# Weight subtractions of a two-block transformer kernel, from VectorE to GpSimd

## The chip, the cores and the metric

The kernel runs on one core of one Trainium2 chip. The metric is the device time of one execution in microseconds (us). Its engines are TensorE (PE in the profile, with PEld for its weight loads), VectorE (DVE), ScalarE (ACT), GpSimd (POOL) and SyncE (SP), which here issues the DMA transfers. Each runs its own row of instructions in order, and they meet through semaphores.

## The reference, cut to what matters

One sequence of 256 tokens with 1024 features goes through two blocks, in float32. Shortened:

```python
# block 1
h = rmsnorm(x, norm_mix)
fq, fk, fv, ff, gq, gk, gv, gb, ga, gz, sq, sk, sv, gates = split(h @ w_in)
ya = fox_attention(rmsnorm(fq), rmsnorm(fk), fv, log_sigmoid(ff + bias))    # softmax attention, decaying
yb = rmsnorm(gated_delta_rule(silu(conv(gq, gk, gv)), gb, ga)) * silu(gz)   # chunks of 64, triangular solve
yc = stick_breaking_attention(sq, sk, sv)
x = x + (g0 * (ya @ w_oa) + g1 * (yb @ w_ob) + g2 * (yc @ w_oc)) @ w_out    # g = sigmoid(gates + bias)
x = x + memory_cross_attention(rmsnorm(x), rmsnorm(mem), w_mq, w_mkv, w_mo)
a, b = split(causal_conv3(rmsnorm(x) @ w_up) + conv_b)                      # 2 x 2816 channels
x = x + (silu(a) * b) @ w_down
# block 2
q, k, v, g, gb, gc, u = split(rmsnorm(x) @ w_in_2)
x = x + concat(silu(g) * groupnorm(retention(rotary(q), rotary(k), v)), gb * conv(gc * u)) @ w_o_2
x = x + moe(rmsnorm(x))               # 64 experts in 8 groups, 2 per token, each 1024 -> 512 -> 1024
return rmsnorm(x, final)
```

## The kernel before, in words

Data stay in SBUF with features on the 128 partitions and the 256 tokens beside each other. The dense weights of everything but the experts are cut into 101 *units* (the list `UNITS`, in the order of use), each 128x2048 float32, 1 MB. Examples: `gq0`, `fv1` (projections), `ga00` (gates), `oa_0` (output projections), `U12` (a column of 128 channels of both halves of `w_up`), `D4` (256 rows of `w_down`), `o200` to `o211` (`w_o_2`).

A product is made in a faster number format, fp32r, in three passes. Each weight W is split as W = high + low, where high is W rounded to fp32r, and each input likewise; then high·high, high·low and low·high are added in PSUM (the function `product`, lines 281 to 283). A unit takes 48 matmuls. Four engines work at a unit one after the other:

1. SyncE issues its load into one of `RAW` = 5 buffers (`raw`), once the unit five before it is multiplied (`done`).
2. ScalarE rounds it into one of `HIGH` = 3 buffers `w_high` (line 871, in `ahead`), once the unit three before it is multiplied, and raises the semaphore `w_high`.
3. VectorE subtracts: `w_low` = `raw` − `w_high`, written over `raw` (line 1354, in `lows`), and raises the semaphore `w_low`.
4. TensorE waits for `w_low` in `parts` and multiplies.

Steps 2 and 3 have no queue of their own. Calls of `ahead(name)` and `lows(name)` stand by hand between the other work of ScalarE and VectorE, and each makes the units up to the one that is named. So a subtraction starts when VectorE's row comes to it, even if its rounded half has long been there, and what stands behind it in the row starts 2.29 us later.

VectorE's other work before the experts: `normalise` (`inverse_root`, then eight multiplications and four low parts `h_low`), roots and products per head, the convolutions' taps, and `split` (a cast to the high part, then a subtraction for the low part, lines 1344 and 1345). In the feed-forward stage a channel column c goes: `up(c)` on TensorE; the tap copy `f_y` on ScalarE (line 1183), which then rounds a unit; taps on VectorE (line 1683); Silu on ScalarE (line 1190); `product(c)` on VectorE, which is `f_act`, the cast `act_high` and the subtraction `act_low`. VectorE takes `product(c - 1)` behind the taps of c. TensorE's order is `up(2j+2)`, `up(2j+3)`, `down(j)`, and `down(j)` needs columns 2j and 2j+1. GpSimd has no work of the program.

Behind the dense units come the router and the 64 experts, whose weights (6 MB each) SyncE loads in three sets of buffers. Expert 0 is loaded in part earlier; `load_gate_up(1, 1)` waits until the last unit is multiplied.

Of the kernel before, what the change touches and what calls it, by code (L numbers as in the profile page):

```python
# [14 lines left out]
ALU = mybir.AluOpType  # L15
# [10 lines left out]
D = 1024  # L26
# [52 lines left out]
def program(nc, c1_in, c2_in, sm_in, rb_in, x_in, mem_in, dense_in, rows_w_in, router_w_in, experts_in, out):  # L79
    with ExitStack() as ctx:  # L80
# [1225 lines left out]
        def _(dve):  # L1306
# [39 lines left out]
            H_PARTS = (h_high, h_low)  # L1346
            w_next = [0]

            def lows(name, n=0):

                while w_next[0] <= min(ORDER[name] + n, LAST):
                    w = UNITS[w_next[0]]
                    dve.wait_ge(sem("w_high"), w_next[0] + 1)
                    V.tensor_tensor(low(w), raw[:, place(w), :], high(w).bitcast(F32),  # L1354
                                    ALU.subtract).then_inc(sem("w_low"), 1)
                    w_next[0] += 1

            dve.wait_ge(sem("consts_loaded"), 32)
            dve.wait_ge(sem("x_loaded"), 16)
            lows(UNITS[0])  # L1360
            normalise("mix", x, A["h"], "norm_mix", H_PARTS)
            lows("gk0")

# [6 lines left out]
            for nm, first in (("gq", 0), ("gk", H), ("gv", 2 * H)):  # L1370
                for u in range(2):
                    ps = half(proj.wait(dve, f"{nm}{u}"))
                    nu += 1
                    dve.wait_ge(sem("gdn_tap"), nu)
                    for s in (1, 2, 3):
                        for i in range(2):
                            ch = first + 2 * u + i
                            o = conv_dst(ch)[:, s:T]
                            ins = V.scalar_tensor_tensor(o, ps[:, i, 0:T - s], S_("gdn_conv", 4 * ch + 3 - s), o,
                                                         ALU.mult, ALU.add)  # L1380
                            if s == 3:
# [5 lines left out]
                    lows(f"{nm}{u}", HIGH)  # L1387

# [15 lines left out]
                            ALU.subtract).then_inc(sem("gdn_tail"), 1)  # L1404
            lows("fk1")


            for hd in range(H):
# [5 lines left out]
                                ALU.mult).then_inc(sem("gdn_k"), 1)  # L1414
            lows("fv0")

# [8 lines left out]
                            ALU.mult).then_inc(sem("gdn_beg"), 1)  # L1425
            lows("fv1")

            for q in range(2):
# [10 lines left out]
                aux.release(dve, f"decay{q}")  # L1439
            lows("sq0")  # L1440

            for nm, gain in (("q", A["st"][:, 24:25]), ("k", S_("fox_k"))):
                for hd in range(H):
                    rs = sq[:, (0 if nm == "q" else H) + hd, :]
                    inverse_root(rs)
                    o = A[f"fox_{nm}"][:, hd, :]
                    V.scalar_tensor_tensor(o, o, gain, rs, ALU.mult, ALU.mult).then_inc(sem(f"fox_{nm}n"), 1)
                lows("sq1" if nm == "q" else "sk0")

            for t in range(TT):  # L1450
                for q in range(2):
# [8 lines left out]
                    aux.release(dve, f"kk{t}{q}")  # L1460
            lows("sk1")
            V.tensor_tensor(A["gdn_qk"][:, :, 0, :], A["gdn_qk"][:, :, 0, :], A["eg"], ALU.mult)
# [55 lines left out]
            for lv in range(len(LEVELS)):  # L1518
                if lv < 5:
                    lows(("sv0", "sv1", "ga00", "ga01", "oa_0")[lv])  # L1520
# [75 lines left out]
            sbout = lambda hd: head_out("spv", hd, yc, "yc")  # L1596
            state(0); sb_keep(0); sb_keep(1); lows("ga11"); mix("a", 0, 0); vnew(1); mix("a", 0, 1); sb_masked(0)
            state(1); sb_masked(1); lows("oa_1"); sbout(0); mix("a", 1, 0); lows("gc00"); sbout(1); vnew(2); mix("a", 1, 1)
            lows("gc01")
            sb_keep(2); sb_keep(3); state(2); sb_masked(2); sb_masked(3); vnew(3); lows("oc_0"); sbout(2); sbout(3)  # L1600
            lows("gc10")
            mix("c", 0, 0); lows("gc11"); mix("c", 0, 1)
            for hd in range(H):
                if hd == 2:
                    lows("oc_1")
# [6 lines left out]
            lows("gb00")  # L1612
            mix("c", 1, 0); lows("gb01"); mix("c", 1, 1)
            lows("gb10")
            mix("b", 0, 0); lows("gb11"); mix("b", 0, 1); lows("ob_1")
            mix("b", 1, 0); lows("out01"); mix("b", 1, 1); lows("out10")

# [9 lines left out]
            residual(("out00", "out01"), "x1")  # L1627
            lows("out11")
            normalise("mem", M["mem"], M["mem"], "norm_mem", hm)
            lows("mk0")  # L1630
            residual(("out10", "out11"), "x1", 2)
            lows("mq0")
            normalise("xq", x, M["mem"], "norm_xq", H_PARTS)
            lows("mv0")
            V.tensor_scalar(M["st"][:, 24:25], S_("mq"), SCALE, None, ALU.mult)
# [7 lines left out]
            mem_norm("k", S_("mk"), range(H))  # L1643
            lows("mv1")
            mem_norm("q", M["st"][:, 24:25], (0, 1))
            lows("mo_0")

# [17 lines left out]
            mem_norm("q", M["st"][:, 24:25], (3,))  # L1665
            mem_max(2); mout(0); mem_norm_p(2); mem_max(3); mout(1); lows("mo_1"); mem_norm_p(3); mout(2); mout(3)
            lows("U0")
            residual(("mo0", "mo1"), "x2")
            lows("U1")
            residual(("mo2", "mo3"), "x2", 2)  # L1670


            normalise("ffn", x, M["mem"], "norm_ffn", H_PARTS)
            lows("U2")

# [19 lines left out]
            for c in range(FC + 1):  # L1695
                if c < FC:
                    taps(c)
                if c:
                    product(c - 1)
                if c < FC:  # L1700
                    lows(f"U{c}", HIGH)
                if c % 2 and c < FC:
                    lows(f"D{c // 2}")
            for b in range(4):
# [6 lines left out]

            lows("q21")
            normalise("n1", x, R["cat"], "norm1", H_PARTS)
            lows("v20")
            dve.wait_ge(sem("c2_loaded"), 16)
# [12 lines left out]
            rotary("q")  # L1728
            lows("gc20")
            rotary("k")  # L1730
            lows("gc21")

# [8 lines left out]
            for hd in range(H):  # L1741
                ret_decay(hd)
                if hd % 2:
                    lows(f"u2{hd // 2}")
            lows("gb20")
            def conv_in(u):
# [9 lines left out]
            for hd in range(H):  # L1756
# [4 lines left out]
                dve.sem_inc(sem("ret_d"), 1)  # L1761
            lows("gb21")
            conv_in(1)
            lows("g20")

# [9 lines left out]
            for hd in range(H):  # L1775
# [3 lines left out]
                link(V.scalar_tensor_tensor(o, o, S_("ret_gn", hd), rs, ALU.mult, ALU.mult))  # L1779
            lows("g21")  # L1780
            for u in range(2):
# [4 lines left out]
                split(cat[0][:, c, :], cat[1][:, c, :], o).then_inc(sem("cat"), 2)  # L1786
            lows("o200")
            for hd in range(H):
                if hd == 2:
                    lows("o201")  # L1790
# [3 lines left out]
            lows("o210")  # L1794
            residual(("o200",), "x4")
            lows("o211")
            residual(("o201", "o210", "o211"), "x4", 1)

# [128 lines left out]
            for k in range(DC):  # L1927
                V.scalar_tensor_tensor(h[:, k, :], x[:, k, :], S_("final", k), sq[:, 0, :], ALU.mult,
                                       ALU.mult).then_inc(sem("result"), 1)


# [217 lines left out]
```

## Time and profile before

| | us |
|---|---|
| median of 3 runs | 1758.27 (1757.1 to 1759.49) |
| the profiled execution, its own time | 1757.1 |
| its span in the profile | 1755.3 |
| TensorE busy | 1354.2 |
| VectorE busy | 647.4 |
| ScalarE busy | 482.1 |
| GpSimd busy | 0.2 |

A row of the page's or the trace's groups names the line of the program, the engine, the operation, `out<-in` by the program's names, and the shapes; `x` is a count. Behind a bar stand the group's busy time, the mean of one in ns, and the idle time of its engine just before, with what ended it (`<-`). In a timeline the first number is the start in us from the span's start, the second the length; what stands in brackets is idle time before the instruction and its releaser. The columns of a stretch are its length, then for each engine busy us and instructions, the granted TensorE clock as a share of full speed, the busy share of the DMA engines and GB/s. A matmul is shown with a length of 0.28 us, but since matmuls overlap, the distance between two starts is the time one takes.

### The profile page before, as it was taken

What the parts mean: (1) busy time and instruction counts of PE and PEld (TensorE: products, weight loads), DVE (VectorE), ACT (ScalarE), POOL (GpSimd) and SP (SyncE); (2) the same over time, 40 slices, a digit from 0 to 9 for tenths busy, and PEclk for the clock granted to TensorE, in tenths of its full rate; (3) what the DMA queues carried; (4) which work ended last, traced back from release to release, by engine and by line L of the source; (5) the groups of instructions that cost most, each with busy time, mean ns of one, the idle gap of its engine ahead of it and who ended that gap; (6) DMA issues with size and microseconds to landing.
All of it is one profiled execution on the core that took longest, in us unless ns stands there. A gap on an engine that the chain in (4) does not pass through costs nothing.

```text
span 1755.3 us, 31165 instructions
## 1 busy us (share of the span) xinstructions
PE 1354.2 (77%) x13670; PEld 1064.1 (61%) x13670; DVE 647.4 (37%) x993; ACT 482.1 (27%) x783; POOL 0.2 (0%) x4
## 2 busy tenths in 40 slices
PE   7998899999799998997766566666665666566665
PEld 6987899989699998987433333333333333333333
DVE  6785635858677776574100010101000100010002
ACT  5773366446455444442000000000000000000001
POOL 0000000000000000000000000000000000000000
PEclk9999999999999999997988897888887988888888
DMA  7432023444265553475899999999999999999995
GB/s 285 166 121 97 25 97 108 158 167 144 73 231 180 182 191 121 148 307 217 366 431 431 430 430 430 430 431 430 431 431 432 432 430 430 431 432 430 430 430 223
DMA packets 34773, 517.27 MB, mean 295 GB/s; under 512 B 3858, under 2 KB 3986, under 8 KB 4882
## 3 DMA queue, kind: packets, MB, share of 16 engines
q1 hardware_dynamic: 34706, 516.32, 72.2%
q8 instruction: 50, 0.82, 0.2%
q14 instruction: 17, 0.14, 0.0%
HBM read 515.25 MB, written 1.05 MB: 294 GB/s over the span
## 4 chain that ended last, share of the span: by engine, by line
PE 45%; DMA 40%; DVE 10%; ACT 3%; issue 1%; SPq 0%; DVEq 0%; ACTq 0%
DMA e_gu<-experts 39%; PE psum L770 11%; PE psum L281 9%; PE psum L282 9%; PE psum L283 9%; DVE all_sq L1322 3%; DVE w_low L1354 2%; PE psum L487 1%; PE psum L340 1%; ACT w_high L871 1%; PE psum L471 1%; PE psum L806 0%; DMA w_raw<-dense 0%; DVE m_sq L1322 0%; PE psum L779 0%
## 5 line engine op out<-in xcount | busy, mean ns | idle before, releaser
L770 PE MATMUL psum<-e_gu,x_xt 128*32 128x256 f32 x4096 | 298.7, 456 | 245.9 <-DMA e_gu<-experts 231.2
L770 PEld LDWEIGHTS psum<-e_gu,x_xt 128*32 128x32 f32 x4096 | 147.2, 130 | 389.3 <-DMA e_gu<-experts 254.2
L281 PE MATMUL psum<-h_high,w_high 128*128 128x256 f32 x1024 | 296.0, 289 | 24.2 <-DVE h_low L1332 15.2
L282 PE MATMUL psum<-h_low,w_high 128*128 128x256 f32 x1024 | 291.6, 285 | 0.0
L283 PE MATMUL psum<-h_high,w_low 128*128 128x256 f32 x1024 | 291.4, 285 | 0.0
L1354 DVE TENSOR_TENSOR w_low<-w_raw,w_high 128x2048 fp32r<-128x2048 f32 x101 | 230.8, 2289 | 56.6 <-ACT w_high L871 50.5
L281 PEld LDWEIGHTS psum<-h_high,w_high 128*128 128x128 f32 x1024 | 196.9, 192 | 27.7 <-issue 16.3
L871 ACT ACTIVATE w_high<-w_raw 128x2048 fp32r<-128x2048 f32 x101 | 193.1, 1914 | 68.8 <-PE psum L283 58.3
L282 PEld LDWEIGHTS psum<-h_low,w_high 128*128 128x128 f32 x1024 | 197.3, 193 | 0.4 <-issue 0.2
L283 PEld LDWEIGHTS psum<-h_high,w_low 128*128 128x128 f32 x1024 | 197.2, 193 | 0.0
L1914 DVE COPY x_yb<-psum 128x256 f32<-128x256 f32 x64 | 27.2, 425 | 429.5 <-PE psum L806 429.5
L1912 DVE TENSOR_TENSOR x_act<-x_sil,psum 128x128 f32<-128x128 f32 x64 | 18.3, 285 | 349.1 <-ACT x_sil L1294 349.1
L806 PE MATMUL psum<-e_dn,x_actT 128*32 128x256 f32 x2048 | 123.8, 382 | 28.8 <-ACT x_actT L1298 28.8
L1294 ACT ACTIVATE x_sil<-psum 128x128 f32<-128x128 f32 x64 | 17.9, 279 | 444.7 <-PE psum L770 444.7
L1296 ACT ACTIVATE x_scat<-psum 128x256 f32<-128x256 f32 x64 | 24.6, 384 | 305.0 <-PE psum L796 303.2
L806 PEld LDWEIGHTS psum<-e_dn,x_actT 128*32 128x32 f32 x2048 | 60.0, 109 | 75.5 <-ACT x_actT L1298 42.5
L812 PE MATMUL psum<-x_scat,x_yb 32*128 32x256 f32 x1024 | 73.3, 400 | 35.0 <-DVE x_yb L1914 35.0
L812 PEld LDWEIGHTS psum<-x_scat,x_yb 32*128 32x128 f32 x1024 | 46.2, 184 | 67.2 <-DVE x_yb L1914 65.8
L779 PE MATMUL psum<-x_s,x_htok 128*128 128x128 f32 x512 | 64.3, 286 | 2.7 <-DVE x_s L1863 2.7
L779 PEld LDWEIGHTS psum<-x_s,x_htok 128*128 128x128 f32 x512 | 61.2, 199 | 7.9 <-issue 5.0
L1322 DVE RECIPROCAL all_sq<-all_sq 128x256 f32<-128x256 f32 (+1 forms) x27 | 53.6, 1987 | 23.7 <-ACTq L850 20.3
L281 PE MATMUL psum<-act_high,w_high 128*128 128x256 f32 x176 | 49.5, 281 | 1.5 <-DVE act_low L1345 1.5
(403 smaller groups left out, 1808.3 us busy)
## 6 DMA issues: line engine op xcount, KB each, us to landing
e_gu<-experts SPq DMA_DIRECT2D x64, 4096.0 KB, 23.8
e_dn<-experts SPq DMA_DIRECT2D x64, 2048.0 KB, 25.3
w_raw<-dense SPq DMA_DIRECT2D x101, 1024.0 KB, 4.8
all_c<-c SPq DMA_DIRECT2D x1, 2099.5 KB, 15.8
r_c<-c SPq DMA_DIRECT2D x1, 1344.0 KB, 5.7
all_x<-x_t SPq DMA_DIRECT2D x1, 1024.0 KB, 5.0
m_mem<-mem_t SPq DMA_DIRECT2D x1, 1024.0 KB, 4.8
out_t<-all_h SPq DMA_DIRECT2D x4, 256.0 KB, 2.6
```

Of the source, the lines that this page charges most:

```text
L281: mm(ps, w[0], src[0], start=start, stop=False, **kw)
L282: mm(ps, w[0], src[1], start=False, stop=False, **kw)
L283: return mm(ps, w[1], src[0], start=False, stop=stop, **kw)
L770: last = mm(half(psum[32 * s:32 * s + 32, GU_BANK[j % 2], 0:256], P), X["xt"][:, k, CAP * j:CAP * (j + 1)], expert_gu[PLACE[j]][:, k, :, s ...
L779: last = mm(psum[:, 4 + c // 4, (c % 4) * P:(c % 4 + 1) * P], X["htok"][:, t, c * P:(c + 1) * P], X["s"][:, t, :], start=(t == 0), stop=(t ...
L806: last = mm(psum[32 * s:32 * s + 32, 7, 0:256], X["actT"][:, CAP * c:CAP * (c + 1)], expert_dn[PLACE[j]][:, c, s * T:(s + 1) * T], start=( ...
L812: last = mm(psum[:, s, d * T:(d + 1) * T], X["yb"][32 * s:32 * s + 32, d * P:(d + 1) * P], X["scat"][32 * s:32 * s + 32, :], start=False, ...
L871: ac(high(w), raw[:, place(w), :], ACT.Copy).then_inc(sem("w_high"), 1)
L1296: ac(X["scat"], psum[:, 7, 256:512], ACT.Copy).then_inc(sem("scatter_kept"), 1)
L1322: link(V.reciprocal(rs, rs))
L1354: V.tensor_tensor(low(w), raw[:, place(w), :], high(w).bitcast(F32), ALU.subtract).then_inc(sem("w_low"), 1)
L1914: V.tensor_copy(X["yb"], psum[:, 7, 0:256]).then_inc(sem("e_y"), 1)
```

## The change

The subtraction of step 3 leaves VectorE. GpSimd gets a row of its own that holds nothing else: for each unit in order it waits for `w_high` and subtracts, with the same operands and the same semaphore behind it. The function `lows` and all of its calls go; where a call stood between two parts of one loop or one list, these are joined. TensorE's, ScalarE's and SyncE's rows stay. The diff, of whose calls taken out a few stand for all:

```diff
-            w_next = [0]
-
-            def lows(name, n=0):
-
-                while w_next[0] <= min(ORDER[name] + n, LAST):
-                    w = UNITS[w_next[0]]
-                    dve.wait_ge(sem("w_high"), w_next[0] + 1)
-                    V.tensor_tensor(low(w), raw[:, place(w), :], high(w).bitcast(F32),
-                                    ALU.subtract).then_inc(sem("w_low"), 1)
-                    w_next[0] += 1
...
-            lows(UNITS[0])
             normalise("mix", x, A["h"], "norm_mix", H_PARTS)
-            lows("gk0")
...
-                lows("sq1" if nm == "q" else "sk0")
...
-                if c < FC:
-                    lows(f"U{c}", HIGH)
-                if c % 2 and c < FC:
-                    lows(f"D{c // 2}")
...
-            residual(("o200",), "x4")
-            lows("o211")
-            residual(("o201", "o210", "o211"), "x4", 1)
+            residual(("o200", "o201", "o210", "o211"), "x4")
...
+        @block.gpsimd
+        def _(pool):
+
+            for n, name in enumerate(UNITS):
+                pool.wait_ge(sem("w_high"), n + 1)
+                nc.gpsimd.tensor_tensor(low(name), raw[:, place(name), :], high(name).bitcast(F32),
+                                        ALU.subtract).then_inc(sem("w_low"), 1)
```

On VectorE, in the feed-forward stage, the row before held a subtraction behind each column (`f_y` are the taps, `f_act` to `act_low` the product):

```order
L1354 TENSOR_TENSOR w_low<-w_raw,w_high 128x2048
L1683 SCALAR_TENSOR_TENSOR f_y<-psum,all_sm,f_y 128x255 x2
L1683 SCALAR_TENSOR_TENSOR f_y<-psum,all_sm,f_y 128x254 x2
L1693 TENSOR_TENSOR f_act<-f_sa,f_y 128x256
L1344 CAST act_high<-f_act 128x256
L1345 TENSOR_TENSOR act_low<-f_act,act_high 128x256
L1354 TENSOR_TENSOR w_low<-w_raw,w_high 128x2048
```

The row of the changed kernel at the same place:

```order
L1647 SCALAR_TENSOR_TENSOR f_y<-psum,all_sm,f_y 128x255 x2
L1647 SCALAR_TENSOR_TENSOR f_y<-psum,all_sm,f_y 128x254 x2
L1657 TENSOR_TENSOR f_act<-f_sa,f_y 128x256
L1344 CAST act_high<-f_act 128x256
L1345 TENSOR_TENSOR act_low<-f_act,act_high 128x256
```

The two subtractions are gone, and the five others follow each other as they did.

On VectorE, between the first attention's keys (`a_fox_k`) and the triangular solve, before:

```order
L1322 RECIPROCAL all_sq<-all_sq 128x256
L1447 SCALAR_TENSOR_TENSOR a_fox_k<-a_fox_k,all_sm,all_sq 128x256
L1354 TENSOR_TENSOR w_low<-w_raw,w_high 128x2048
L1458 TENSOR_TENSOR a_kd<-psum,a_t 128x256 x8
L1354 TENSOR_TENSOR w_low<-w_raw,w_high 128x2048
L1462 TENSOR_TENSOR a_gdn_qk<-a_gdn_qk,a_eg 128x4x256
L1467 TENSOR_TENSOR all_sq<-a_kd,all_c_58 128x1024
```

And now:

```order
L1322 RECIPROCAL all_sq<-all_sq 128x256
L1430 SCALAR_TENSOR_TENSOR a_fox_k<-a_fox_k,all_sm,all_sq 128x256
L1440 TENSOR_TENSOR a_kd<-psum,a_t 128x256 x8
L1443 TENSOR_TENSOR a_gdn_qk<-a_gdn_qk,a_eg 128x4x256
L1448 TENSOR_TENSOR all_sq<-a_kd,all_c_58 128x1024
```

The chain to the first solve (`all_sq` is the masked matrix that it starts from) is two subtractions shorter. All 101 of them stand in GpSimd's row:

```order
L1881 TENSOR_TENSOR w_low<-w_raw,w_high 128x2048 x101
```

## Rows read from the trace of the kernel before

**Rows 1.** Page, part 1: busy us (share of the span) x instructions.
```profile
PE 1354.2 (77%) x13670; PEld 1064.1 (61%) x13670; DVE 647.4 (37%) x993; ACT 482.1 (27%) x783; POOL 0.2 (0%) x4
```

**Rows 2.** Stretches; stretch, its length, then columns as headed.
```profile
core 0: us, PE busy (x) PEld busy (x) DVE busy (x) ACT busy (x) POOL busy (x), PEclk, DMA share, GB/s
0.00:800.00 800.00, 738.84 (x5706) 712.04 (x5707) 539.09 (x676) 404.84 (x551) 0.20 (x4) 0.97 0.44 155
480.00:660.00 180.00, 179.26 (x1515) 179.06 (x1514) 133.34 (x185) 88.95 (x99) 0.00 (x0) 1.00 0.56 192
800.00:1755.00 955.00, 615.41 (x7965) 352.03 (x7963) 108.30 (x318) 77.30 (x232) 0.00 (x0) 0.85 0.96 412
```

**Rows 3.** Page, part 4: chain that ended last, shares by line.
```profile
DMA e_gu<-experts 39%; PE psum L770 11%; PE psum L281 9%; PE psum L282 9%; PE psum L283 9%; DVE all_sq L1322 3%; DVE w_low L1354 2%; PE psum L487 1%; PE psum L340 1%; ACT w_high L871 1%; PE psum L471 1%; PE psum L806 0%; DMA w_raw<-dense 0%; DVE m_sq L1322 0%; PE psum L779 0%
```

**Rows 4.** Timeline of TensorE; start us, us, engine line op out<-in.
```profile
567.52 0.28 PE L281 MATMUL psum<-act_high,w_high 128*128 128x256 f32 x1
...
573.20 0.28 PE L281 MATMUL psum<-h_high,w_high 128*128 128x256 f32 x1
```

**Rows 5.** Waits of TensorE, 0 to 810: us in total, times, longest us.
```profile
PE psum L281 <- DVE w_low L1354: 13.7, 7, 3.1
...
PE psum L281 <- DVE act_low L1345: 1.5, 1, 1.5
```

**Rows 6.** Groups by line and form, VectorE, 0 to 810; busy us, mean ns.
```profile
L1354 DVE TENSOR_TENSOR w_low<-w_raw,w_high 128x2048 fp32r<-128x2048 f32 x101 | 230.8, 2289 | 56.6 <-ACT w_high L871 50.5 <-DVE a_s L1571 0.6 <-DVE all_x L1622 0.5
...
L1345 DVE TENSOR_TENSOR act_low<-f_act,act_high 128x256 fp32r<-128x256 f32 x22 | 9.4, 426 | 0.8
L1693 DVE TENSOR_TENSOR f_act<-f_sa,f_y 128x256 f32<-128x256 f32 x22 | 9.4, 425 | 7.8 <-ACT f_sa L1190 7.0 <-DVE f_y L1683 0.8
...
L1344 DVE CAST act_high<-f_act 128x256 fp32r<-128x256 f32 x22 | 6.5, 294 | 0.8
```

**Rows 7.** Timeline of VectorE, first attention.
```profile
120.74 1.75 DVE L1322 RECIPROCAL all_sq<-all_sq 128x256 f32<-128x256 f32 x1
...
122.92 2.28 DVE L1354 TENSOR_TENSOR w_low<-w_raw,w_high 128x2048 fp32r<-128x2048 f32 x1
...
139.67 2.29 DVE L1354 TENSOR_TENSOR w_low<-w_raw,w_high 128x2048 fp32r<-128x2048 f32 x1
```

**Rows 8.** Timeline of VectorE, ahead of o200.
```profile
761.35 2.29 DVE L1354 TENSOR_TENSOR w_low<-w_raw,w_high 128x2048 fp32r<-128x2048 f32 x1
...
771.73 2.28 DVE L1354 TENSOR_TENSOR w_low<-w_raw,w_high 128x2048 fp32r<-128x2048 f32 x1
```

**Rows 9.** Timeline of ScalarE, feed-forward stage.
```profile
562.04 1.02 ACT L1183 ACTIVATE f_y<-psum,all_sm 128x256 f32<-128x256 f32 x2 [3.70 <-PE psum L283]
562.95 1.91 ACT L871 ACTIVATE w_high<-w_raw 128x2048 fp32r<-128x2048 f32 x1
564.75 0.41 ACT L1190 ACTIVATE f_sa<-f_y 128x256 f32<-128x256 f32 x1
```

**Rows 10.** Timeline of VectorE, feed-forward stage.
```profile
565.27 0.43 DVE L1693 TENSOR_TENSOR f_act<-f_sa,f_y 128x256 f32<-128x256 f32 x1 [0.32 <-ACT f_sa L1190]
565.73 0.29 DVE L1344 CAST act_high<-f_act 128x256 fp32r<-128x256 f32 x1
566.06 0.43 DVE L1345 TENSOR_TENSOR act_low<-f_act,act_high 128x256 fp32r<-128x256 f32 x1
566.40 2.29 DVE L1354 TENSOR_TENSOR w_low<-w_raw,w_high 128x2048 fp32r<-128x2048 f32 x1
```

**Rows 11.** Timelines of ScalarE and VectorE, the first instructions.
```profile
13.14 0.47 ACT L848 ACTIVATE all_sq<-psum,all_c 128x256 f32<-128x256 f32 x1 [0.25 <-PE psum L340]
...
11.52 2.29 DVE L1354 TENSOR_TENSOR w_low<-w_raw,w_high 128x2048 fp32r<-128x2048 f32 x1 [11.52 <-ACT w_high L871]
13.77 1.75 DVE L1322 RECIPROCAL all_sq<-all_sq 128x256 f32<-128x256 f32 x1
```

**Rows 12.** Timeline of VectorE, a cast out of PSUM.
```profile
190.46 0.42 DVE L1344 CAST ya_high<-psum 128x256 fp32r<-128x256 f32 x1
```

More of the change, by code:

```diff
@@ L1386, in _ @@
                     proj.release(dve, f"{nm}{u}")
-                    lows(f"{nm}{u}", HIGH)
             dve.wait_ge(sem("late_consts_loaded"), 16)
@@ L1404, in _ @@
                             ALU.subtract).then_inc(sem("gdn_tail"), 1)
-            lows("fk1")
             for hd in range(H):
@@ L1414, in _ @@
                                 ALU.mult).then_inc(sem("gdn_k"), 1)
-            lows("fv0")
             ps = aux.wait(dve, "tok")
@@ L1425, in _ @@
                             ALU.mult).then_inc(sem("gdn_beg"), 1)
-            lows("fv1")
             for q in range(2):
@@ L1439, in _ @@
                 aux.release(dve, f"decay{q}")
-            lows("sq0")
             for nm, gain in (("q", A["st"][:, 24:25]), ("k", S_("fox_k"))):
@@ L1460, in _ @@
                     aux.release(dve, f"kk{t}{q}")
-            lows("sk1")
             V.tensor_tensor(A["gdn_qk"][:, :, 0, :], A["gdn_qk"][:, :, 0, :], A["eg"], ALU.mult)
@@ L1518, in _ @@
             for lv in range(len(LEVELS)):
-                if lv < 5:
-                    lows(("sv0", "sv1", "ga00", "ga01", "oa_0")[lv])
                 between()
@@ L1596, in _ @@
             sbout = lambda hd: head_out("spv", hd, yc, "yc")
[L1597 to L1602, printed above, removed]
+            state(0); sb_keep(0); sb_keep(1); mix("a", 0, 0); vnew(1); mix("a", 0, 1); sb_masked(0)
+            state(1); sb_masked(1); sbout(0); mix("a", 1, 0); sbout(1); vnew(2); mix("a", 1, 1)
+            sb_keep(2); sb_keep(3); state(2); sb_masked(2); sb_masked(3); vnew(3); sbout(2); sbout(3)
+            mix("c", 0, 0); mix("c", 0, 1)
             for hd in range(H):
-                if hd == 2:
-                    lows("oc_1")
                 rs = sq[:, hd, :]
@@ L1611, in _ @@
                 split(yb[0][:, hd, :], yb[1][:, hd, :], o).then_inc(sem("yb"), 1)
[L1612 to L1616, printed above, removed]
+            mix("c", 1, 0); mix("c", 1, 1)
+            for hf in range(2):
+                for p in range(2):
+                    mix("b", hf, p)
             def residual(names, done, n=0):
@@ L1627, in _ @@
             residual(("out00", "out01"), "x1")
-            lows("out11")
             normalise("mem", M["mem"], M["mem"], "norm_mem", hm)
-            lows("mk0")
             residual(("out10", "out11"), "x1", 2)
-            lows("mq0")
             normalise("xq", x, M["mem"], "norm_xq", H_PARTS)
-            lows("mv0")
             V.tensor_scalar(M["st"][:, 24:25], S_("mq"), SCALE, None, ALU.mult)
@@ L1643, in _ @@
             mem_norm("k", S_("mk"), range(H))
-            lows("mv1")
             mem_norm("q", M["st"][:, 24:25], (0, 1))
-            lows("mo_0")
             def mem_max(hd):
@@ L1665, in _ @@
             mem_norm("q", M["st"][:, 24:25], (3,))
[L1666 to L1670, printed above, removed]
+            mem_max(2); mout(0); mem_norm_p(2); mem_max(3); mout(1); mem_norm_p(3); mout(2); mout(3)
+            residual(("mo0", "mo1", "mo2", "mo3"), "x2")
             normalise("ffn", x, M["mem"], "norm_ffn", H_PARTS)
-            lows("U2")
             def taps(c):
@@ L1709, in _ @@
                 dve.sem_inc(sem("x3"), 1)
-            lows("q21")
             normalise("n1", x, R["cat"], "norm1", H_PARTS)
-            lows("v20")
             dve.wait_ge(sem("c2_loaded"), 16)
@@ L1728, in _ @@
             rotary("q")
-            lows("gc20")
             rotary("k")
-            lows("gc21")
             def ret_decay(hd):
@@ L1742, in _ @@
                 ret_decay(hd)
-                if hd % 2:
-                    lows(f"u2{hd // 2}")
-            lows("gb20")
             def conv_in(u):
@@ L1761, in _ @@
                 dve.sem_inc(sem("ret_d"), 1)
-            lows("gb21")
             conv_in(1)
-            lows("g20")
             for u in range(2):
@@ L1779, in _ @@
                 link(V.scalar_tensor_tensor(o, o, S_("ret_gn", hd), rs, ALU.mult, ALU.mult))
-            lows("g21")
             for u in range(2):
@@ L1786, in _ @@
                 split(cat[0][:, c, :], cat[1][:, c, :], o).then_inc(sem("cat"), 2)
-            lows("o200")
             for hd in range(H):
-                if hd == 2:
-                    lows("o201")
                 dve.wait_ge(sem("ret_g"), hd // 2 + 1)
@@ L1793, in _ @@
                 split(cat[0][:, hd, :], cat[1][:, hd, :], R["cat"][:, hd, :]).then_inc(sem("cat"), 1)
-            lows("o210")
-            residual(("o200",), "x4")
-            lows("o211")
-            residual(("o201", "o210", "o211"), "x4", 1)
+            residual(("o200", "o201", "o210", "o211"), "x4")
             normalise("n2", x, h, "norm2")
```

## The prediction

> **What bounds the kernel now.** I read the busy times of the engines first: GpSimd does nothing (0.2 us), VectorE is busy 37% of the span [rows 1]. Then a table of stretches: up to 800 us TensorE is busy 739 us while the DMA engines are busy 44%; behind it they are busy 96% at 412 GB/s [rows 2]. So there are two kernels in one. The second part (64 experts) is bound by the transfer of the expert weights; the chain of waits gives it 39% of the span [rows 3]. The change puts no instruction there: its last subtraction belongs to the last dense unit, `o211`. But most of the expert transfers are issued only when the dense units are multiplied, so each us won or lost before 800 us moves the end by about one.
>
> The first part is TensorE at work on 101 weight units, 48 matmuls each. In the feed-forward stage it never stops (179.3 of 180 us) [rows 2], and a unit takes 5.68 us: the first matmul of D4 at 567.52, that of the next unit at 573.20 [rows 4]. What it waits for in this part, by TensorE's own waits: 13.7 us in 7 waits for `w_low`, the result of the subtraction that the change moves, and only 1.5 us, once, for `act_low`, which VectorE makes of the activation [rows 5]. The 101 subtractions cost VectorE 230.8 us, 2.29 us each [rows 6].
>
> **The change part by part.** *VectorE loses* 101 × 2.29 = 231 us of its 539 busy us before 800 us [rows 2, 6]. Only some of it is on TensorE's path. (a) The 13.7 us of direct waits: a subtraction stood in VectorE's row behind other work while its rounded half was long there. GpSimd's row holds nothing else, so these go: −13.7. (b) Thirteen subtractions stand inside VectorE chains for which TensorE waits. The first is at 122.92, among the roots and products of the first attention, with two more behind it to 139.67 [rows 7]; the last three are at 761.35 to 771.73, ahead of `o200` [rows 8]; the other seven lie in the same way in the gated output, the mixing and the memory attention. They are 13 × 2.29 = 30 us of VectorE. TensorE has multiplications of its own beside about half of it, so this is worth −15, with bounds 0 and −30. What is late next in these chains are the RECIPROCALs (1.75 us each) [rows 7] and TensorE itself.
>
> *GpSimd gains* 101 subtractions of 128x2048. The trace shows it at no such work, so rows of other engines bound the price: not under VectorE's 2.29 us; if it takes its two inputs one after the other at VectorE's pace, 2 × 2.29 = 4.6; if the two inputs and the output go one after the other, 3 × 2.29 = 6.9. I take 4.6, since ScalarE needs 1.91 us for one input of this size [rows 9], and two of those with a start are 4. The Trainium skill, "GPSIMD Engine Reference", section Performance versus the Vector engine, gives 4497 ns for such a tensor_tensor against 2293 ns on VectorE; the second agrees with the row, the first is shown by no run yet, and by it the sum would be the same within 1 us.
>
> At 4.6 us GpSimd keeps up with one unit each 5.68 us. The latency is hidden too, as ScalarE rounds a unit three units ahead: in the feed-forward stage U12's rounding starts at 562.95 and ends at 564.87, and its product starts at 573.20 [rows 4, 9]. That is 8.3 us for a step of 4.6, so 3.7 are left. Where ScalarE rounds late, a unit comes 4.6 − 2.29 = 2.3 us later; since VectorE's freedom lets ScalarE round earlier, I take 0, bounds 0 and +5.
>
> *The first instructions.* VectorE's first row is now the RECIPROCAL. It started at 13.77, behind the subtraction of 11.52, and its input is there at 13.6 [rows 11], so it gains 0.2 us. In exchange the next subtractions run beside the normalisation. Bounds −0.2 and +4.6; I take +2.
>
> *What runs beside what.* This is the term that decides. Until now no instruction of GpSimd met one of VectorE. In this trace a cast of 128x256 takes 0.42 us out of PSUM [rows 12] and 0.29 us from SBUF to SBUF [rows 6]: VectorE has a second way into SBUF. If GpSimd's traffic takes that way, a VectorE instruction with two SBUF inputs, or a fast copy, may have to wait until the running subtraction is over. Bounds for one such instruction: 0 and 4.6 us. The feed-forward stage alone has 66 of them (`f_act`, cast, `act_low`, 22 each) [rows 6].
>
> See what it would do there [rows 4, 9, 10]. The end of an `up` unit releases on ScalarE the tap copy (562.04), the rounding (562.95 to 564.87) and the Silu (to 565.16). VectorE's three steps to the halves of the activation, `f_act`, cast and `act_low`, run from 565.27 to 566.49, and TensorE needs them at 567.52: 1.03 us of slack. Today the subtraction stands behind them (566.40), by program order. On GpSimd it starts when the rounding ends, 564.9, so 0.4 us ahead of `f_act`, and holds the way until 564.9 + 4.6 = 569.5. Then come the 1.22 us of the three steps: 570.7. TensorE, ready at 567.5, waits 3.2 us. Nothing is rounded meanwhile, so nothing blocks the second and third step. This repeats at each of the 11 `D` units: 11 × 3.2 = +35. Bounds: 0, and if two of the three steps each meet a subtraction, 11 × 7.8 = 86.
>
> In the chains of (b) the same blocking takes the gain back: about 17 subtractions fall into these stretches, and each stops VectorE for what does not lie under a RECIPROCAL, 4.6 − 1.75 = 2.8 us. That is 48 us against the 30 that leave, net +18, of which TensorE sees half: +9 in place of −15, bounds −15 and +18.
>
> I take the blocking as real. It is also the Trainium skill's rule: "SBUF — State Buffer", section Who interferes with whom, says that a VectorE instruction with two SBUF inputs contends with a GpSimd instruction that reads SBUF, and that whoever comes second is blocked for the whole of the other's instruction. The trace has no moment with both engines at work, so it neither confirms nor denies this; by the rule the time is the forecast below, without it the first rival.
>
> The sum stands against the profiled execution, whose own time is 1757.1 us (span 1755.3), 1.2 under the median of the runs: direct waits −13.7, feed-forward +35, chains +9, start +2, together +32. Forecast: 1757.1 + 32 = 1789 us.
>
> **The rivals.**
> *Faster: the two engines do not hinder each other.* Then −13.7 direct, −15 in the chains, −1.5 for the one wait for `act_low`, +2.3 for one unit rounded late: near −28, 1729 us. For it: nothing in the rows but the faster cast speaks for a shared way, and the ring of three rounded units gives each subtraction 8 us. Against it: that cast. It decides if `f_act` is held up by less than the slack of 1.03 us.
> *Slower still: GpSimd needs 6.9 us.* Above 5.68 us GpSimd is the bound wherever units follow without a gap: 33 in the feed-forward stage and about 20 elsewhere. 53 × (6.9 − 5.68) = +64, −13.7 direct, 0 for the chains: +50, 1807 us, and 1830 or more if it also blocks VectorE. For it: the output is fp32r, a rounded write that GpSimd does nowhere in this trace. Against it: it would take three passes at VectorE's pace.
> *No change: a finer sharing.* Each engine is slowed only by the time in which both want the way. In the feed-forward stage that is 9.4 + 6.5 + 9.4 = 25 us of VectorE's instructions [rows 6], so a step of 0.43 us becomes 0.9 and uses up the slack, no more; gain and loss are 10 to 20 us each. 1757 ± 10.
> That the change doesn't do what it says can be excluded by the new order: 101 subtractions on GpSimd, none on VectorE, TensorE's rows the same.
>
> **How the numbers follow.** Blocked for whole instructions: 0.52 (own range 1770 to 1815: a subtraction of 4.0 to 5.2 us moves the stage by 11 × 0.6 either way, and the chains are known to about ±15). Free of each other: 0.30 (1720 to 1745). Slow GpSimd: 0.11 (1795 to 1850). Finer sharing: 0.07. The range 1728 to 1816 leaves out half of the slow case, the better half of the free one and the tails. A measurement of this kernel can tell 0.2%, 3.5 us, from no change: faster is 0.30 and about half of the finer sharing, 0.33; same 0.04; slower 0.63.
>
> **What would show it.** Right: on GpSimd 101 TENSOR_TENSORs of 4 to 5 us that start at the end of `w_high`; in the feed-forward stage `f_act` held up by about 4 us, TensorE waiting for `act_low` 11 times for some 3 us, and its busy share down from 100% to about 85%; no more waits for `w_low`; instructions that read PSUM, as the taps `f_y`, as long as before; the experts' part as long as before. Wrong: `f_act` at 0.43 us beside a running subtraction (then the free case, and the dense units, now at their end near 800 us, end near 772 and not 832), or subtractions of over 5.7 us with TensorE waiting for `w_low` in the feed-forward stage.

## The result, and the profile after

The changed kernel takes 1819.61 us (median of 4 runs, 1817.98 to 1821.52) against 1758.35 us (1757.1 to 1759.49): ratio 1.034, 95% interval 1.0333 to 1.0357, so 61 us slower. The forecast was 1789 us with a range of 1728 to 1816. The sign was right; the size was missed by 31 us, and the time lies outside the range.

The page of the changed kernel begins so (part 1; busy us, share of the span, instructions):

```profile
span 1818.5 us, 31166 instructions
PE 1376.0 (76%) x13669; PEld 1083.1 (60%) x13670; DVE 597.4 (33%) x892; ACT 480.7 (26%) x783; POOL 466.7 (26%) x105
```

Against [rows 1]: VectorE has 101 instructions fewer, worth 230.8 us, but is only 50 us less busy. The other 181 us are time in which an instruction had started and stood (below: it was *held*). TensorE is busy 21.8 us more with the same matmuls. GpSimd, by line and form (count, busy us, mean ns):

```profile
L1881 POOL TENSOR_TENSOR w_low<-w_raw,w_high 128x2048 fp32r<-128x2048 f32 x101 | 466.5, 4623 | 384.0 <-ACT w_high L871 383.9
```

4.62 us each; I had taken 4.6. The stretches that answer to [rows 2] (the same view, after the change), TensorE alone (length, busy us, count, granted clock, DMA share, GB/s):

```profile
0.00:863.00 863.00, 760.88 (x5706) 0.93 0.41 144
525.00:705.00 180.00, 178.34 (x1487) 1.00 0.55 191
863.00:1818.00 955.00, 615.11 (x7965) 0.85 0.96 412
```

The same 5706 matmuls need 863 us instead of 800: 22.0 us more of TensorE's busy time at a lower granted clock (0.93 in place of 0.97), 41 us more of waiting. The experts' part is the same to 0.3 us. The feed-forward stage runs at 99% busy, where I had expected 85%. TensorE's waits, 0 to 870 us, answer to [rows 5]:

```profile
PE psum L281 <- DVE h_low L1332: 22.5, 4, 9.2
PE psum L281 <- DVE cat_low L1345: 10.8, 3, 9.8
PE psum L471 <- issue: 9.8, 4, 5.0
PE psum L471 <- DVE all_sq L1448: 9.7, 1, 9.7
...
PE psum L281 <- DVE act_low L1345: 8.7, 12, 4.4
PE psum L614 <- DVE m_q L1612: 8.0, 1, 8.0
PE psum L281 <- DVE mixed_low L1345: 7.4, 2, 6.6
PE psum L281 <- POOL w_low L1881: 5.6, 2, 5.2
```

The waits for `w_low` fell from 13.7 to 5.6 us. What grew are waits for VectorE's other results. VectorE by line and form (answers to [rows 6]) shows why:

```profile
L1657 DVE TENSOR_TENSOR f_act<-f_sa,f_y 128x256 f32<-128x256 f32 x22 | 80.6, 3662 | 8.2 <-ACT f_sa L1190 4.5 <-DVE f_y L1647 3.7
...
L1345 DVE TENSOR_TENSOR act_low<-f_act,act_high 128x256 fp32r<-128x256 f32 x22 | 18.3, 830 | 0.8
...
L1344 DVE CAST act_high<-f_act 128x256 fp32r<-128x256 f32 x22 | 6.5, 294 | 0.8
```

The same 22 `f_act` took 9.4 us before and take 80.6 now; none takes less than 2.5 us. Two of the 22 `act_low` met a subtraction too (4.87 us each). One `f_act`, first in VectorE's timeline (answers to [rows 10]), then the subtraction in GpSimd's (start us, us):

```profile
611.40 4.58 DVE L1657 TENSOR_TENSOR f_act<-f_sa,f_y 128x256 f32<-128x256 f32 x1 [0.32 <-ACT f_sa L1190]
616.01 0.29 DVE L1344 CAST act_high<-f_act 128x256 fp32r<-128x256 f32 x1
616.34 0.43 DVE L1345 TENSOR_TENSOR act_low<-f_act,act_high 128x256 fp32r<-128x256 f32 x1
```

```profile
611.08 4.62 POOL L1881 TENSOR_TENSOR w_low<-w_raw,w_high 128x2048 fp32r<-128x2048 f32 x1 [1.64 <-ACT w_high L871]
```

The subtraction starts 0.32 us ahead and ends at 615.70; `f_act` ends 0.28 us behind it. By the Trainium skill ("SBUF — State Buffer", Who interferes with whom) the one that comes second is blocked for the whole of the other's instruction: the trace agrees, 4.58 us beside 4.62.

TensorE hardly notices it. Its timeline in this unit, D4 (answers to [rows 4]): the first matmul, the last two of the first 24, and the first of the second 24:

```profile
613.65 0.28 PE L281 MATMUL psum<-act_high,w_high 128*128 128x256 f32 x1
...
616.25 0.28 PE L282 MATMUL psum<-act_low,w_high 128*128 128x256 f32 x1
616.37 0.28 PE L283 MATMUL psum<-act_high,w_low 128*128 128x256 f32 x1
616.82 0.39 PE L281 MATMUL psum<-act_high,w_high 128*128 128x256 f32 x1 [0.17 <-DVE act_low L1345]
```

It starts D4 at once and needs the halves that VectorE makes (ready at 616.77) only at 616.49, behind the first 24 matmuls. The unit takes 6.11 us instead of 5.68.

Where TensorE lost it: the end of a unit's last matmul, after minus before, from the two traces (below: the *shift* at that unit).

| unit ends at | gq0 | fv0 | sk0 | ga00 | ga10 | oc_1 | ob_0 | out00 | mv1 | mo_0 | D0 | D9 | D10 | g21 | o200 |
|---|---|---|---|---|---|---|---|---|---|---|---|---|---|---|---|
| us | 4.8 | 3.0 | 7.3 | 30.0 | 25.7 | 25.3 | 29.4 | 33.2 | 46.9 | 43.4 | 44.8 | 48.7 | 56.1 | 55 | 63.2 |

The largest step, 22.7 us from sk0 to ga00, is the triangular solve of the delta rule with the fox attention beside it, a stage in which no direct wait and hardly a subtraction on the path had been booked.

### The profile page after: what moved, and what is told of

Same layout as the page of the kernel before. It is cut to its first block, busy times and chain, and to the rows that moved or that the text cites. A ratio compares the mean times of both kernels' runs of the same rounds, so it can differ in the third digit from the quotient of the medians.

```text
span 1818.5 us, 31166 instructions
## 1 busy us (share of the span) xinstructions
PE 1376.0 (76%) x13669; PEld 1083.1 (60%) x13670; DVE 597.4 (33%) x892; ACT 480.7 (26%) x783; POOL 466.7 (26%) x105
## 4 chain that ended last, share of the span: by engine, by line
DMA 38%; PE 37%; DVE 17%; ACT 4%; issue 2%; POOL 1%; SPq 0%; DVEq 0%; ACTq 0%
DMA e_gu<-experts 38%; PE psum L770 10%; PE psum L281 6%; PE psum L282 6%; PE psum L283 6%; DVE f_act L1657 3%; DVE all_sq L1322 3%; ACT w_high L871 1%; DVE f_y L1647 1%; PE psum L340 1%; PE psum L471 1%; DVE m_mem L1335 1%; DVE r_qraw L1730 1%; PE psum L487 1%; DVE act_low L1345 1%
## 5 line engine op out<-in xcount | busy, mean ns | idle before, releaser
L1881 POOL TENSOR_TENSOR w_low<-w_raw,w_high 128x2048 fp32r<-128x2048 f32 x101 | 466.5, 4623 | 384.0 <-ACT w_high L871 383.9
L1657 DVE TENSOR_TENSOR f_act<-f_sa,f_y 128x256 f32<-128x256 f32 x22 | 80.6, 3662 | 8.2 <-ACT f_sa L1190 4.5
```

Source lines behind the costliest of these rows:

```text
L1657: link(V.tensor_tensor(F["act"][:, c % 2, :], F["sa"][:, c % 3, :], F["y"][:, c % 3, 1, :], ALU.mult))
L1881: nc.gpsimd.tensor_tensor(low(name), raw[:, place(name), :], high(name).bitcast(F32), ALU.subtract).then_inc(sem("w_low"), 1)
```

## The experiments

Beside each the kernel before was timed again: its medians are 1758.0 to 1759.6 us. Differences are taken from that median.

**Which stage.** Two kernels divide the change: the units U0 to D10 (feed-forward) on GpSimd and the others on VectorE as before, and the reverse. In both, each engine counts its own units:

```
                    if not on_pool(w):          # VectorE's subtraction, as before
...
            for n, name in enumerate(UNITS):    # GpSimd's loop
                if on_pool(name):
```

> GpSimd subtracts only the 33 units of the feed-forward stage (U0 to D10); VectorE keeps the other 68 in their old places. Theory A (a VectorE instruction with two SBUF inputs waits for the whole running subtraction, but a D unit starts with the column that was ready long before, 24 of its 48 matmuls or 2.84 us, so TensorE sees only 4.3 - 1.03 - 2.84 = 0.4 us per D unit and 7.4 at D10, whose order needs both columns early): 10 x 0.43 + 7.4 = +12 us over the kernel before, 1770 us. Theory B (the forecast's price, 3.2 us at each of 11 D units): +35, 1793 us. Theory C (no blocking, GpSimd is only slower): within 3 us of 1758.

Measured: 1765.2 us (1764.1 to 1767.0), ratio 1.0040 (1.0026 to 1.0054), +7.

> The complement: GpSimd subtracts the 68 units outside the feed-forward stage, VectorE the 33 inside. Theory A (the loss lies in the serial VectorE chains before and behind the stage): the changed kernel's +61 less 12, +49, 1807 us, with TensorE's clock below full in the solve stage as in the changed kernel. Theory B (the stage costs 35): +26, 1784 us.

Measured: 1817.04 us, ratio 1.0330 (1.0313 to 1.0348), +59. The feed-forward stage alone costs 7, not 35. In the whole change the shift grows by 12 over it (U0 to D10), as the last products are also held by the subtractions of q20 and q21. At D10 the shift grows by 7.4 in the whole change, 2.8 with the stage alone and 8.2 with the rest alone: most of the 5 us by which 7 + 59 exceed 61 lie there. The rest, which I had booked at −3, costs nearly all.

**Why the stage of 11 blocks costs little.** Unit Dj multiplies the column of the even activation first and the late one second (24 matmuls each, 2.84 us). This kernel turns the order round in the changed kernel, and a control does it in the kernel before (both activations are then given back together, at the unit's end; D10 keeps its order):

```
-                steps = [(c, n) for c in range(2) for n in range(DC)]
+                steps = [(c, n) for c in ((0, 1) if ends else (1, 0)) for n in range(DC)]
```

> The changed kernel, but each D unit except D10 multiplies its later column (2j+1) first and the earlier one second. Same work. Theory A: without the 2.84 us of the ready column the wait per D unit becomes 4.3 - 1.03 = 3.27 in place of 0.43, so 10 x 2.84 = +28 us over the changed kernel, 1848 us; TensorE's waits for act_low total some 33 us more. Theory C (the order inside a unit does not matter, and f_act's blocked time is hidden otherwise): within 4 us of 1820.

Measured: 1848.73 us, ratio 1.0520 (1.0500 to 1.0539), 29 us over the changed kernel. TensorE's waits, 500 to 760 us:

```profile
PE psum L281 <- DVE act_low L1345: 30.5, 10, 3.1
```

> Control: the same order of columns in the kernel before, with the subtractions on VectorE. act_low was ready 1.03 us before the unit began, so all theories expect no change, 1758 us within 4; a loss would mean that the order costs something by itself.

Measured: 1758.22 us, ratio 1.0001 (0.9991 to 1.0010). So the 3.2 us of my estimate were right, and stood behind 2.84 us of work that I had not seen: 10 × 0.43 us are left. That the total came near the 28 us expected is in part luck. By its shifts the kernel with the order turned round is 36 us behind the changed one at D9: 28 from the ten waits and 8 more in D0, D5, D6 and D9, whose matmuls ran slower behind the wait (D5: 8.30 us instead of 5.68). At D10 it gets 9 back.

**The solve.** The changed kernel with the six units sk1 to oa_0 kept on VectorE:

> The changed kernel, but the six units sk1 to oa_0, whose subtractions run beside the triangular solve and the fox attention, stay on VectorE. Theory A (each of these GpSimd subtractions blocks one instruction of the serial chain): from sk0 to ga00 TensorE lost 22.7 us in the changed kernel; with these six gone it loses at most 3, so 1799 us (1795 to 1805). Theory B (the stage is late from a lower TensorE clock that the earlier stages left behind): no more than 5 us come back, 1815 us.

Measured: 1799.94 us, ratio 1.0231 (1.0214 to 1.0248): 20 us come back, theory A. The other way, from the kernel before:

> The kernel before with only the six units sk1 to oa_0 on GpSimd. Theory A (these six make the stage's loss by themselves): 20 us (17 to 23) are lost, 1778 us. Theory B (the stage's loss needs the lateness from earlier stages too): under 12 us, 1768 us.

Measured: 1776.03 us, ratio 1.0098 (1.0081 to 1.0115), +18: theory A. VectorE's timeline of this stretch, four instructions in the kernel before and the same four in the changed one:

```profile
141.88 1.22 DVE L1462 TENSOR_TENSOR a_gdn_qk<-a_gdn_qk,a_eg 128x1024 f32<-128x1024 f32 x1
...
158.24 1.23 DVE L1467 TENSOR_TENSOR all_sq<-a_kd,all_c 128x1024 f32<-128x1024 f32 x1 [0.24 <-DVE a_u L1473]
...
171.18 0.17 DVE L1489 TENSOR_SCALAR a_st<-a_st 128x2 f32<-128x2 f32 x1
...
189.32 1.23 DVE L1467 TENSOR_TENSOR all_sq<-a_kd,all_c 128x1024 f32<-128x1024 f32 x1 [0.25 <-DVE a_u L1473]
```

```profile
153.28 4.61 DVE L1443 TENSOR_TENSOR a_gdn_qk<-a_gdn_qk,a_eg 128x1024 f32<-128x1024 f32 x1
...
173.09 3.81 DVE L1448 TENSOR_TENSOR all_sq<-a_kd,all_c 128x1024 f32<-128x1024 f32 x1 [0.24 <-DVE a_u L1454]
...
191.35 3.48 DVE L1470 TENSOR_SCALAR a_st<-a_st 128x2 f32<-128x2 f32 x1
...
214.55 3.07 DVE L1448 TENSOR_TENSOR all_sq<-a_kd,all_c 128x1024 f32<-128x1024 f32 x1 [0.25 <-DVE a_u L1454]
```

Together they are held 11.1 us. TensorE lost twice that, 22.7 us. The stretches of the stage say how (matmuls, granted clock), the kernel before and then the changed one:

```profile
142.00:220.00 78.00, 68.77 (x521) 63.24 (x520) 45.93 (x72) 31.20 (x78) 0.00 (x0) 0.98 0.16 55
```

```profile
149.00:250.00 101.00, 78.26 (x523) 71.52 (x522) 50.20 (x76) 31.14 (x78) 18.50 (x5) 0.85 0.13 42
```

The same matmuls took 9.5 us longer, at a granted clock of 0.85 instead of 0.98. Whether GpSimd's traffic does that, or any stop of the chain, is told apart by a kernel without GpSimd work whose chain is longer at the same four places:

```
+                for _ in range({0: 3, 1: 2, 3: 2}.get(lv, 0)):
+                    link(V.tensor_tensor(A["lm"], A["kd"][:, :, 1, :], m, ALU.mult))
...
+                for t, (lo, w) in 4 * list(enumerate(spans)) if pre == "fox" and hd == 0 else ():
+                    link(V.reduce_max(st[:, t:t + 1], s[:, lo:lo + w], AX))
```

> The kernel before, nothing on GpSimd, with VectorE's solve chain made longer at the four places where the changed kernel was held there: the level mask product of levels 0, 1 and 3 is computed three, two and two times more (1.22 us each), and the first fox maximum four times more (about 3 us), some 11.5 us in all against 11.2 us of blocks. Theory A (a stop of the chain costs once as a wait and again through the lower clock that TensorE is granted behind it): TensorE's matmuls of the stage take about 9 us more (granted clock near 0.85 in place of 0.98), 20 to 23 us are lost: 1780 us. Theory B (TensorE is slowed by GpSimd's traffic): the clock stays at 0.98, 11 to 12 us are lost: 1770 us.

Measured: 1779.41 us, ratio 1.0124 (1.0107 to 1.0141): +21.3 for 11.4 us of work (7 × 1.22 and 2.8). The stretch of this stage:

```profile
142.00:239.50 97.50, 77.50 (x521) 70.72 (x520) 58.88 (x86) 30.55 (x77) 0.00 (x0) 0.86 0.13 44
```

Nearly the same clock and the same TensorE time as beside GpSimd, so its traffic isn't needed for the loss. By the shifts 19.3 of the 21.3 us fall between sk0 and ga00. The first stop is paid once: up to sk1 the 3.7 us of added products cost 3.8. The three behind it are paid twice: 7.7 us of added work cost 15.5 from sk1 to ga00, and in the changed kernel 7.8 us of holds cost 15.1. Up to sk1 the changed kernel loses 7.6 us, more than the 3.4 of its first hold; its VectorE came late already from holds in the attention before, as that of the last `a_fox_k` (146.71 for 3.05 us instead of 0.48). So the factor of two is that of the three later stops; over the whole step it is partly chance.

TensorE was 88% busy here at almost the full clock; with a few us more of standing at four places, a larger part of its matmuls runs at the lower of its two levels (1.2 and 2.4 GHz). As only these two are granted, a mean of 0.98 over 78 us is some 3 us at the lower one, and 0.85 over 101 us some 30. The Trainium skill, "TensorE: Matmul & The Clock Gate", Part 1, says that idleness takes the clock to 1.2 GHz and activity releases it; the granted clock of these three rows agrees.

**How long is a block.** If the block ends with the instruction, shorter instructions should cure it. The changed kernel with its subtraction cut into 4, 8 and 16:

```
+                for s in range(4):
+                    c = slice(s * UNIT // 4, (s + 1) * UNIT // 4)
+                    last = nc.gpsimd.tensor_tensor(low(name)[:, c], raw[:, place(name), c], high(name)[:, c].bitcast(F32),
```

> The changed kernel with each of the 101 GpSimd subtractions cut into four of 128x512. Theory A, the block: an instruction of VectorE with two SBUF inputs waits for the GpSimd instruction that is under way, to its end, and no longer. An instruction of 4.62 us becomes four of about 1.2 us, so f_act (mean 3.66 us in the changed kernel) falls to about 1.2 us, the D units find their activations in time, and the solve stage loses about 1 us for each subtraction instead of 4: about 1772 us (1760 to 1785). Theory B, what counts is the total work of GpSimd beside VectorE (101 x 4.6 us), however it is cut: no better than the changed kernel, 1815 to 1825 us. Theory C, the loss is in the lateness of w_low and in TensorE's clock: 1815 us or above, since four instructions are no quicker than one.

Measured: 1779.67 us, ratio 1.0123 (1.0104 to 1.0143): as theory A says, a third of the loss is left. VectorE, by line and form:

```profile
L1345 DVE TENSOR_TENSOR act_low<-f_act,act_high 128x256 fp32r<-128x256 f32 x22 | 30.8, 1398 | 0.8
L1344 DVE CAST act_high<-f_act 128x256 fp32r<-128x256 f32 x22 | 27.9, 1268 | 0.8
L1657 DVE TENSOR_TENSOR f_act<-f_sa,f_y 128x256 f32<-128x256 f32 x22 | 24.0, 1090 | 8.2 <-ACT f_sa L1190 4.5 <-DVE f_y L1647 3.7
```

Each of the three steps now waits for the rest of one piece (1353 ns), the cast too. TensorE loses nothing at D1 to D9; its loss lies in the chains and at D10 (4.8 us).

> The same, cut into sixteen of 128x128. Theory A (the block lasts only to the end of the running instruction): no block over about 0.35 us; f_act near 0.6 us. With each piece at 0.30 us and a start of its own of some tenths, a unit takes 5 to 8 us, which the rings cover in most places. 1740 us if nothing of it is late, 1765 us if the pieces push units late; I take 1750 us. Theory B (total GpSimd work): 1820 us or above. If A holds this is at or below the kernel before, because the direct waits on w_low (13.7 us) are gone.

Measured: 1875.5 us (1858.7 to 1886.1), ratio 1.0642 (1.0572 to 1.0712): a miss, 125 us from what I took. VectorE's and GpSimd's timelines:

```profile
607.44 13.11 DVE L1657 TENSOR_TENSOR f_act<-f_sa,f_y 128x256 f32<-128x256 f32 x1 [0.32 <-ACT f_sa L1190]
620.58 0.43 DVE L1344 CAST act_high<-f_act 128x256 fp32r<-128x256 f32 x1
```

```profile
606.87 14.00 POOL L1883 TENSOR_TENSOR w_low<-w_raw,w_high 128x128 fp32r<-128x128 f32 x33
```

A product of 0.43 us stood 13.11 us, to 620.55, while some thirty pieces ran past it, and went through with the last piece before GpSimd had to stop (620.87). The 22 `f_act` (shortest, median and longest, ns):

```profile
L1657 DVE TENSOR_TENSOR f_act<-f_sa,f_y x22: 425/674/13427, 526.9 to 770.8; 128x256 f32<-128x256 f32 x22
```

Eight took 8.9 to 13.4 us: three ended with the row of pieces, five went through after 22 to 30 pieces while more followed. The other fourteen took 0.43 to 0.75, and eight of these ran beside pieces too. So it doesn't happen each time. Two whole subtractions that followed each other at once didn't do it in the changed kernel (VectorE, then GpSimd):

```profile
388.63 4.66 DVE L1569 TENSOR_TENSOR a_mixed<-a_tmp,a_tmp 128x512 f32<-128x512 f32 x1
393.33 4.60 DVE L1344 CAST mixed_high<-a_mixed 128x512 fp32r<-128x512 f32 x1
```

```profile
388.14 9.50 POOL L1881 TENSOR_TENSOR w_low<-w_raw,w_high 128x2048 fp32r<-128x2048 f32 x2 [1.08 <-ACT w_high L871]
```

`a_mixed` went through when the first ended (392.74), and the second held only the cast behind it. Theory A as I had put it, a block that ends with the running instruction, is false for short pieces. Is it the lack of a gap? In the next kernel GpSimd waits for the end of each piece before it starts another:

```
+                    last.then_inc(sem("piece"), 1)
+                    pool.wait_ge(sem("piece"), 16 * n + s + 1)
```

> Sixteen pieces of 128x128 as before, but GpSimd waits after each piece until that piece has ended before it starts the next. The kernel with sixteen pieces held one f_act of VectorE for 13.11 us while 31 pieces ran back to back. Theory A2 (the SBUF path stays with GpSimd as long as its next instruction is already waiting when one ends; a gap gives VectorE its turn): f_act falls from 4.73 us to under 1 us and the act_low waits of TensorE (59.7 us) go; the units get longer (16 x 0.45 to 0.6 us, 8 to 10 us), which now makes w_low late in places: about 1800 us (1775 to 1830). Theory B (VectorE loses in proportion to the number of GpSimd instructions or to GpSimd's busy time, 717 us): f_act stays at 4 us or above, 1875 us or more.

Measured: 1943.47 us, ratio 1.1053 (1.1036 to 1.1070). The mechanism of A2 is borne out by the group of `f_act` (longest 0.71 us), and its time is missed by 140 us:

```profile
L1657 DVE TENSOR_TENSOR f_act<-f_sa,f_y 128x256 f32<-128x256 f32 x22 | 11.6, 527 | 8.2 <-ACT f_sa L1190 8.2
```

```profile
PE psum L281 <- POOLq L1887: 148.4, 66, 6.7
```

VectorE is nearly free (0.53 us for 0.43), but a unit now takes 8.6 to 8.8 us on GpSimd against 5.68 on TensorE, which waits 148 us for it. I had let the rings cover the longer units, but where the units are made more slowly than TensorE multiplies them, no ring covers it.

> The changed kernel with each subtraction cut into eight of 128x256, back to back. Four pieces (1353 ns each) let VectorE in after one piece, sixteen (444 to 486 ns each) did not. If the length of the piece decides whether the next one is ready in time to keep the path, the eight (about 0.75 us each) may fall on either side: near 1770 us if VectorE gets its turn (f_act under 1 us), above 1830 us if not (f_act over 3 us). A theory in which the block ends with the running instruction whatever its length says 1765 us; I take 1770 us.

Measured: 1795.33 us, ratio 1.0227 (1.0196 to 1.0258): between the two sides. The 22 `f_act` say that it falls on either, as with sixteen:

```profile
L1657 DVE TENSOR_TENSOR f_act<-f_sa,f_y x22: 419/758/12490, 499.1 to 694.6; 128x256 f32<-128x256 f32 x22
```

Mostly VectorE gets its turn after one piece (0.76 us); three are held for 12.0 to 12.5 us, each to the end of a row of pieces, and the shifts of that kernel have three jumps of 10 us, at D2, D5 and D9. What decides between the two is not shown.

**Only where TensorE waits for the subtraction.** Ten units on GpSimd, 91 on VectorE:

> The kernel before, with only ten units on GpSimd (fv0, sq1, sk0, ga10, oc_1, gb00, ob_0, out00, g21, o200: those for which TensorE waited for the subtraction, or nearly); the other 91 stay on VectorE in their places. Theory A (each whole subtraction on GpSimd blocks one instruction of a chain by up to 4.3 us): the 13.7 us of direct waits go, about as much comes back: 1762 us (1750 to 1775). Theory B (only a block in the feed-forward or the solve matters): all of the direct waits are won, 1745 us.

Measured: 1756.45 us, ratio 0.9986 (0.9976 to 0.9996), between the two theories. By the shifts it won at fv0 4.1, sq1 and sk0 3.1, ga10 4.3, oc_1 and gb00 3.7, out00 2.4 us, and lost again at sq0 4.2, sk1 2.3, ga11 1.5, gb01 4.4, mo_0 2.0 and o200 3.4. At gb01 TensorE waits 2.6 us for the next subtraction of VectorE, not moved and now the late one. With three units, whole and in four pieces:

> The kernel before, with three units alone on GpSimd, whole: fv0, ga10 and out00. With ten units on GpSimd TensorE won 4.05 us at fv0, 4.3 at ga10 (1.5 of it lost again at ga11) and 2.4 at out00, and lost 4.15 at sq0 and 3.4 at o200, where the subtractions of sq1, sk0 and o200 held VectorE's instructions. Theory A (each unit stands for itself: the wait won less the instruction held): about 1 to 2 us stay of fv0, since the fox chain behind it waits for VectorE anyway, 2.8 of ga10 and 2.4 of out00, so 1752 us (1750 to 1755). Theory B (the gains depend on each other and the chains behind take them back): 1756 to 1758 us.

Measured: 1755.26 us, ratio 0.9982 (0.9973 to 0.9991).

> The same three units, each in four pieces of 128x512. Theory A: what is held is at most one piece (about 1.35 us) at a time, but the unit takes 5.4 us instead of 4.6; it wins the 1.5 us at ga11 and loses nothing where w_low is early: 1751 us. Theory B: no difference from whole units, within 1 us.

Measured: 1755.02 us, ratio 0.9982 (0.9973 to 0.9991). About 3 us better than the kernel before, and nearer to theory B: the waits for `w_low` fell from 13.7 to 5.4 us, but at sq0 all of fv0's 4 us are gone (TensorE is at +0.8 there), with no subtraction on GpSimd near: the first fox root starts at 113.93 instead of 114.18, so the chain behind had not waited for fv0, and at mo_0 2.2 us of out00's. Splitting changes nothing measurable here.

## Why the prediction was right or wrong

- *GpSimd's step of 4.6 us; the ring hides it.* Right in the size, 4.62 us. The waits for `w_low` fell by 8 of the 13.7 us only: at ob_0, where ScalarE rounds late, TensorE waits 5.2 us.
- *Whole-instruction blocking.* Right in the changed kernel: 4.58 us beside 4.62, and one step each for two long subtractions in a row. "Nothing is rounded meanwhile, so nothing blocks the second and third step" failed twice, at two `act_low` of 4.87 us. By the Trainium skill (same section) the block lasts for the whole of the other's instruction; with short ones back to back the runs show some blocks over some thirty instructions, and the measurement decides.
- *Feed-forward +35.* Wrong. The failed step is "TensorE needs them at 567.52". The late activation is that of the second column, needed 24 matmuls or 2.84 us later, so that about 0.4 of the 3.2 us is left, 0.43 by the units' lengths; with D10 (+7.4) the stage cost 12 us. Turning the columns round brought ten waits of 3.1 us, so the wait itself was sized rightly.
- *The chains +9, bounds −15 and +18.* Wrong, the larger miss: with start and direct waits I had −3, measured are +51 (the shift of 63.2 at o200 less the 11.7 over the feed-forward stage). Two steps failed. I counted the subtractions that stood in chains of the kernel before; on GpSimd they run when ScalarE has rounded, and so beside any instruction of any chain. The solve had hardly one on its path and lost most (22.7 us; shown by keeping its six units on VectorE, and by moving only them). And "of which TensorE sees half" had no row behind it: in the solve the blocks came through whole, and with them some 10 us of slower matmuls (shown without GpSimd by the delayed chain). The remaining 24 us outside (of 51, less 22.7 and the 4.8 of the start) lie in the attention before, the mixing, the memory attention and ahead of o200; they are read from the shifts and from held instructions as `a_mixed`, not tested one by one. Over the kernel TensorE's extra busy time is 22 of the 61 us; that all of it has this cause is read from the granted clock, not tested stage by stage.
- *Start +2.* Measured +4.8, just over its bound of 4.6. Four products of the first normalisation meet the subtraction of gq1 (GpSimd, 16.38 for 4.70 us; answers to [rows 11]):

```profile
16.24 5.91 DVE L1335 SCALAR_TENSOR_TENSOR a_h<-all_x,all_sm,all_sq 128x256 f32<-128x256 f32 x4
```

- The two errors, −23 in the feed-forward stage and +54 outside it, partly cancelled: the total is nearer than either term.
- *Rivals.* Engines free of each other (`f_act` 0.43 us) and a finer sharing (0.9 us) are excluded by the 22 `f_act`, 3.66 us in the mean and none under 2.5, a slow GpSimd by the 4.62 us of the subtraction.

## What to carry to other kernels

Before moving work to GpSimd, list the VectorE instructions with two SBUF inputs, the casts from SBUF and the like on every serial chain that will run beside it, wherever the moved work stood before; each costs up to the length of the GpSimd instruction. Where TensorE and VectorE wait for each other in turn, allow for more than the stop itself: in the solve it was paid once at the first of four places and twice at the three others. In a software pipeline, check which operand the consumer takes first before calling a late one a stall.

## What the runs showed of the hardware

- A VectorE operation needn't be large to be held, nor have two inputs: `a_st`, 128x2, took 3.48 us instead of 0.17, a cast of 128x512 4.60 instead of 0.43. RECIPROCAL (3.35 us) and operations with an input in PSUM (`f_y`, 0.48 us) took as long beside a subtraction as without.
- Back-to-back GpSimd instructions of 0.49 us kept VectorE out for up to 13.4 us at 8 of the 22 `f_act`; of 0.78 us for up to 12.49 at 3 of them; of 1.35 us at none (longest 1.51 us).
- A piece costs more than its share: GpSimd's busy time by 101 units is 4.62 us for the whole, 5.3 in four, 5.9 in eight, 7.1 in sixteen pieces.
